# Output projections of a two-layer encoder: the split of the attention output issued two tiles ahead

## The reference, cut to what matters

```
mp = attention_output @ w_out                       # 1024 x 1024 weights, f32
yp = layer_norm(ALPHA * yp + mp, ln_gain[i, 0], ln_bias[i, 0])
# layer 1 only, ahead of w_out: o = rms_norm(out, subln_g) * (1 - lambda_init)
```

## Time and profile before

| what | value |
|---|---|
| median of 3 runs | 3468.49 us |
| profiled execution, its own time | 3463.33 us |
| its span, first to last instruction | 3461.5 us |
| TensorE busy (matmul) | 3146.9 us, 91% |
| VectorE / ScalarE / GpSimd busy | 45% / 26% / 30% |
| mean granted TensorE clock | 0.954 of full |
| share of L1522 (output projections) in the chain that ended last | 5% |

### The profile page before, as it was taken

One profiled execution on the slowest core, in us unless ns is written; L12 is line 12 of the kernel. 1 busy time (PEld: TensorE's weight loads), 2 busy tenths in 40 slices (PEclk: granted clock), 3 DMA queues, 4 the chain that ended last, 5 costly groups with the idle time before them and its releaser, 6 DMA issues.

```text
span 3461.5 us, 49928 instructions
## 1 busy us (share of the span) xinstructions
PE 3146.9 (91%) x19621; PEld 2929.0 (85%) x19621; DVE 1560.8 (45%) x2880; ACT 887.1 (26%) x1921; POOL 1045.6 (30%) x504
## 2 busy tenths in 40 slices
PE   7896999987999999999968999988799999999996
PEld 7585777765999999999958999966599999999996
DVE  2589754522443334333352555563244333334335
ACT  2355544423101010011122445453311010100112
POOL 2122000123443343333443212212244333433333
PEclk9998899998999999999979999998899999999997
DMA  2121000012111111111112112111111111111111
GB/s 80 34 53 44 1 1 1 32 30 57 43 61 37 42 42 45 52 36 42 42 49 73 46 41 58 34 50 49 42 58 46 52 36 42 42 46 51 36 48 50
DMA packets 209355, 149.48 MB, mean 43 GB/s; under 512 B 28914, under 2 KB 195764, under 8 KB 209236
## 3 DMA queue, kind: packets, MB, share of 16 engines
q1 hardware_dynamic: 209236, 147.85, 14.0%
HBM read 128.09 MB, written 19.73 MB: 43 GB/s over the span
## 4 chain that ended last, share of the span: by engine, by line
PE 83%; DVE 8%; ACT 3%; issue 2%; POOL 1%; DMA 1%; ACTq 0%; SPq 0%; POOLq 0%; DVEq 0%
PE psum L151 46%; PE psum L1901 15%; PE psum L1522 5%; PE psum L612 4%; PE psum L578 2%; PE psum L593 2%; DVE junk L827 2%; PE psum L1186 2%; PE psum L1160 2%; PE psum L1174 1%; DVE h_lo L1978 1%; PE psum L533 1%; PE psum L547 1%; ACT x_newA L1574 1%; DVE ln_part L1769 1%
## 5 line engine op out<-in xcount | busy, mean ns | idle before, releaser
L151 PE MATMUL psum<-x_hi,w_hi 128*128 128x352 f32 (+1 forms) x3192 | 1040.6, 326 | 29.6 <-POOL w_lo L122 13.6
L151 PE MATMUL psum<-x_hi,w_lo 128*128 128x352 f32 (+1 forms) x3192 | 1028.6, 322 | 0.0
L151 PE MATMUL psum<-x_lo,w_hi 128*128 128x352 f32 (+1 forms) x3192 | 1028.3, 322 | 0.0
L120 POOL TENSOR_TENSOR w_hi<-w_raw,zeros 128x1024 fp32r<-128x1024 f32 (+1 forms) x209 | 386.0, 1847 | 1673.8 <-PE psum L151 1419.4
L151 PEld LDWEIGHTS psum<-x_hi,w_hi 128*128 128x128 f32 (+1 forms) x3192 | 602.0, 189 | 31.7 <-issue 21.1
L151 PEld LDWEIGHTS psum<-x_lo,w_hi 128*128 128x128 f32 (+1 forms) x3192 | 602.9, 189 | 0.4
L151 PEld LDWEIGHTS psum<-x_hi,w_lo 128*128 128x128 f32 (+1 forms) x3192 | 602.0, 189 | 0.5
L122 POOL TENSOR_TENSOR w_lo<-w_raw,w_hi 128x1024 fp32r<-128x1024 f32 (+1 forms) x209 | 489.1, 2340 | 16.4
L1973 DVE TENSOR_TENSOR gate<-psum,gate 128x352 f32<-128x352 f32 x132 | 69.2, 525 | 803.1 <-PE psum L151 803.1
L1901 PE MATMUL psum<-h_hi,w_hi 128*128 128x352 f32 x1056 | 344.5, 326 | 51.9 <-DVE h_lo L1978 51.9
L1988 DVE TENSOR_TENSOR o_col<-psum,o_col 128x352 f32<-128x352 f32 x528 | 271.7, 523 | 197.1 <-PE psum L1901 197.1
(11 more groups left out here) (458 smaller groups left out, 4171.1 us busy)
## 6 DMA issues: line engine op xcount, KB each, us to landing
w_raw<-in_ffn_w_dram SPq DMA_DIRECT2D x132, 512.0 KB
w_raw<-in_b_w_in_dram SPq DMA_DIRECT2D x24, 512.0 KB
w_raw<-in_ple_w_gate_dram SPq DMA_DIRECT2D x16, 512.0 KB
x_nat<-in_x_prompt_dram SPq DMA_DIRECT2D x8, 512.0 KB, 3.5
w_raw<-in_a_w_in_dram SPq DMA_DIRECT2D x8, 512.0 KB
w_raw<-in_a_w_in_dram SPq DMA_DIRECT2D x16, 256.0 KB
x_rows<-x_rows SPq DMA_DIRECT2D x8, 512.0 KB, 2.6
out_new_b_v_prompt_dram<-valsB SPq DMA_DIRECT2D x8, 512.0 KB, 3.4
```

Of the source, the lines that this page charges most:

```text
L120: nc.gpsimd.tensor_tensor(c.w_hi[s][:, 0:kc], c.w_raw[s][:, 0:kc], zero, ALU.add).then_inc(c.split[s], 1)
L151: last = c.nc.tensor.matmul(out, w, x, start=(n == 0), stop=(n == 3 * len(terms) - 1))
```

## The change

On ScalarE `o_high` is issued for tile t + 2 at the top of the loop over t, from t = 0 on, where it was issued for tile t + 1 from t = 1 on. On VectorE `o_low(t + 2)` is issued at the end of iteration t, behind the coefficients, where `o_low(t + 1)` stood near its top, ahead of the wait for tile t's matmuls. TensorE's, GpSimd's and SyncE's lists, the buffers and the number of instructions stay as they are. Both kinds are changed.

```diff
@@ scalar
         for t in range(T):
             n = rows(t)
-            if t >= 1 and t + 1 < T:
-                o_high(t + 1)
+            if t + 2 < T:
+                o_high(t + 2)
             act.wait_ge(s_mv, b_mv + t + 1)
@@ vector
             if not A and t + 2 < T:
                 o_scale(t + 2)
-            if t >= 1 and t + 1 < T:
-                o_low(t + 1)
             v.wait_ge(s_mm, b_mm + t + 1)
@@ vector, end of the iteration
             nc.vector.scalar_tensor_tensor(out=coef[0:n, 2:3], in0=mv[0:n, 0:1], scalar=-1.0, in1=coef[0:n, 1:2],
                                            op0=ALU.mult, op1=ALU.mult).then_inc(s_co, 1)
+            if t + 2 < T:
+                o_low(t + 2)
```

## The result

The changed kernel takes 3404.59 us, the median of 4 runs (3403.31 to 3404.77), against 3468.52 us of the kernel before (3468.38 to 3470.33): ratio 0.9814, 95% interval 0.9802 to 0.9827. The forecast was 3405.5 us. The profiled execution took 3404.73 us.

What follows compares the result with a forecast made beforehand. TensorE (83% of the chain) was taken as the bound, idling for late `o_lo` and then slowed by its clock. Savings of 33.8 us (kind A) and 29.0 (kind B), together 62.8, from 3468.49 gave 3405.7, rounded 3405.5 us; range 3400 to 3411.

Steps and rivals of the forecast that it cites:

- Tiles 2 to 7 go at tile 1's length: Both output projections: six tiles of 11.81 us in kind A, 12.68 in kind B, saving 33.8 and 29.0 us.
- The split left the path: `o_low` ends 5.8 to 6.6 us after a tile's matmuls, before TensorE wants it, so the wait goes in both kinds.
- The clock follows the waits: TensorE in tiles 2 to 7: granted clock 1.00 without long waits, removing 1.7 us of slow matmuls per tile period.
- first rival: Both projections: waits go but the slow clock stays, only 41.3 us of idle time saved, 3427 us; chance 0.07.
- the slower one: Both projections: six dense tiles in a row run at 1.2 GHz, 61 us more, 3530 us; chance 0.03.
- The new place of `o_high` is covered: ScalarE: the root queued behind `o_high(t+2)` costs nothing; the other end was 1.31 us in 14 places, 18 us.
- E: The time at which tile t's matmuls end on TensorE; the forecast counts later events from it.
- second rival: Kind B: late root makes `turn_back` hold TensorE in mid-tile, so kind B gains nothing, 3434.7 us; chance 0.04.
- the 3.3 us in kind A: Lateness hidden between the normalization's end at E + 4.9 and `turn_back`'s need of it at E + 8.2.
- its bounds of 2.08 and 2.91: `o_low` on VectorE: 2.08 us as in the chain, at worst 2.91, its longest row, beside GpSimd's work.
- Carrying the difference to the median over: The runs' median lay 5.16 us above the profiled execution; the forecast kept this, 3405.7 instead of 3400.5 us.

Runs made afterwards that it cites:

- filling the wait: Kernel before, with 12 unused 128 x 512 matmuls behind tiles 1 to 6 of kind A, in the wait for `o_lo`: 3459.56 us, ratio 0.9973.
- four more copies: Changed kernel, with 4 more copies of the same tile ahead of each of `o_high(2)` to `o_high(7)` in kind A on ScalarE: 3402.27 us, ratio 0.9804.
- six more copies: Changed kernel, with 6 more copies of the same tile ahead of each of `o_high(2)` to `o_high(7)` in kind A on ScalarE: 3414.61 us, ratio 0.9844.

## Why the prediction was right

- **Tiles 2 to 7 go at tile 1's length.** 11.81 us were worked out for kind A, 11.79 measured; 12.68 for kind B, 12.70 (tiles 1 to 5). A tile in the same trace that happened to have no wait was the right measure, since it held the clock as well as the work.
- **The split left the path.** `o_low` was to end 5.8 to 6.6 us after the tile's matmuls in kind A and at 6.6 in kind B; behind tile 1 it ends at 5.95 and 6.13, and TensorE doesn't wait for it.
- **The clock follows the waits.** Said from the rows, shown in kind A by filling the wait: 9.7 us of its 34.0. The first rival (slow matmuls stay, 3427 us) and the slower one (dense work at 1.2 GHz, 3530 us) both fall with the clock of 1.00.
- **The new place of `o_high` is covered.** Kind B's `o_high` ends 0.56 us before the root's turn (2.5 against 2.96 after E had been worked out), and no row of TensorE waits at L1501 within a tile: the second rival falls.
- **The normalization ends 1.2 us later than in the forecast.** The normalization of tile t was to end at E + 4.9; it ends at E + 6.1 (719.69 + 1.24 against 714.84), for the coefficient waits for `x_lo`. In the old order VectorE did `o_low` ahead of the residual, and the coefficient came after `x_lo`'s end (719.00 against 718.06 in the trace of before); now VectorE begins with the residual at once, and the coefficient falls beside `x_lo`. So 2.1 of the 3.3 us in kind A are left between it and `turn_back`. A later `o_high` doesn't add to this: with four more copies the coefficient starts at 723.38, behind `x_lo`'s end at 722.10, and takes 0.16 us again. `o_low` came out shorter than its bounds of 2.08 and 2.91, at 1.21, for it starts when GpSimd is done; the two errors nearly cancel in the time at which it ends.
- **What I missed without harm: the table load.** The first root of kind A needs ScalarE's table of functions. In the trace of before that load stood in idle time (at 689.38, with the root at 703.56); now it stands behind `o_high(2)`:

```profile
703.23 1.06 ACT L1537 ACTIVATE o_hi0A<-o_col 128x1024 fp32r<-128x1024 f32 x1 [11.52 <-PE psum L1522]
704.31 1.28 ACT L1564 ACT_TABLE_LOAD   x1
705.99 0.29 ACT L1564 ACTIVATE ln_coefA<-ln_mvA,eps 128x1 f32<-128x1 f32 x1 [0.40 <-DVE ln_mvA L1631]
```

  It ends 0.40 us before the root can run. With more copies ahead of it the same load is on the path of the first place: it is all of the 0.6 us wait with four, and with six it makes that place 1.4 us dearer than the others (wait of 2.8 against 1.4 us).
- **VectorE's edit was read as part of the gain, and isn't.** I costed "VectorE issues `o_low(t+2)` behind the coefficients" as if it were the new place. In kind A the end of one iteration and the top of the next are the same place in a list: nothing moves. In kind B it passes `o_scale(t+3)` only. The sum wasn't touched by this, the reading of the change was.
- **The rest of the span.** The profiled execution of before was 5.2 us under its median, that of after was at it. 58.6 us lie between the two profiled executions, 62.9 in the stretches; 4.3 us were lost again elsewhere (2.4 of them ahead of kind A's tile 1, the rest wasn't looked for). Carrying the difference to the median over, and not the profiled time, was right here. That the forecast is within 1 us of the result is in part luck: a second set of runs has 3471.20 and 3404.43 us, a saving of 66.8 where the first has 63.9, and 62.8 was worked out. The firm agreement is that of the stretches.

## What to carry to other kernels

When a buffer has two copies, look in the in-order list of each engine for what refills it: an instruction that needs nothing new, but stands behind one that waits for the current tile, costs a wait per tile, and placing it ahead by one iteration costs nothing while the instruction that it passes is itself waiting. Price the result by a tile of the same trace that had no wait, clock included, and read the end of one iteration and the top of the next as one place. Where instructions move in time, ask which instructions of VectorE with two SBUF inputs now fall beside GpSimd's.

## What the runs showed of the hardware that I hadn't expected

- A `scalar_tensor_tensor` of 128 x 1 with both tensor inputs in SBUF, started within a GpSimd `tensor_tensor` of 128 x 1024, lasted until that had ended (1.33 us instead of 0.16); `tensor_scalar` in its place, with one of the two as a scalar per row, took 0.21.
- Waits of 3.0 to 3.3 us ahead of a tile brought slow matmuls in most places (granted clock 0.90 of a tile) but not in all: one in the kernel with kind B alone changed passed at 1.00 (kind A's tile 2, period 15.38 us instead of 17.0). Waits of 0.57 us and of 1.4 us, once per tile, never did (1.00 over 61.54 and 53.77 us), nor did the single one of 2.8 us with six more copies (1.00 over that tile, and the next has the period of the others, 13.46 us).
